# Gate and up projections of an FFN as seven block products for eight, with the gated chunks kept in DRAM until all down projections run last

## What is computed

```python
def swiglu(x, w_gate, w_up, w_down):
    return (jax.nn.silu(x @ w_gate) * (x @ w_up)) @ w_down

def run_trunk(h, p, conv_bufs, past, ...):
    for i in range(DEPTH):
        ...                       # conv mixer or attention, h = h + rmsnorm(y, norm_g[i, 1])
        h = h + rmsnorm(swiglu(rmsnorm(h, norm_g[i, 2]), w_gate[i], w_up[i], w_down[i]), norm_g[i, 3])
        h = h + jax.nn.sigmoid(h @ w_ple_gate[i]) * (p[i] @ w_ple[i])
```

## Time and profile before

| | us |
|---|---|
| median of 3 runs | 3127.33 (3124.76 to 3129.07) |
| span of the profiled execution | 3127.3 |
| TensorE busy | 3075.6 (98%) |
| VectorE busy | 1567.8 (50%) |
| ScalarE busy | 903.5 (29%) |
| GpSimd busy | 262.2 (8%) |
| chain that ended last: TensorE's share | 82% |
| matmuls of the three lines L2273 to L2275 on `xs`, each | 845 to 849 busy |

### The profile page before, as it was taken

How to read it: one execution, slowest core, us unless ns; L and a number is a source line. 1 busy time by engine, 2 the same in 40 slices (tenths; PEclk the granted TensorE clock), 3 DMA queues, 4 the chain that set the end, 5 groups by cost and what they waited for, 6 DMA issues and landing times.

```text
span 3127.3 us, 51548 instructions
## 1 busy us (share of the span) xinstructions
PE 3075.6 (98%) x20352; PEld 2942.6 (94%) x20352; DVE 1567.8 (50%) x2613; ACT 903.5 (29%) x1600; POOL 262.2 (8%) x317
## 2 busy tenths in 40 slices
PE   8999999999999999999999999999999999999999
PEld 8999999999999999999977886569999999999998
DVE  5444284444444447453335665553744444444472
ACT  4111351111111116332235553343411111111262
POOL 1000010000000001000015551110100000000011
PEclk9999999999999999999999999999999999999999
DMA  3111111111111121113257865961111111111112
GB/s 107 45 44 47 42 39 43 48 41 48 46 42 48 41 62 41 41 48 112 98 154 160 162 119 222 395 249 40 42 44 46 48 41 48 41 48 47 57 48 71
DMA packets 229210, 247.46 MB, mean 79 GB/s; under 512 B 19061, under 2 KB 183925, under 8 KB 228994
## 3 DMA queue, kind: packets, MB, share of 16 engines
q1 hardware_dynamic: 204978, 164.65, 17.7%
q0 software_dynamic: 24016, 79.77, 8.3%
...
## 4 chain that ended last, share of the span: by engine, by line
PE 82%; DVE 4%; issue 2%; ACT 1%; DMA 1%; POOL 0%; SPq 0%; DVEq 0%; ACTq 0%; POOLq 0%
PE psum L2273 20%; PE psum L2275 20%; PE psum L2274 20%; PE psum L2857 2%; PE psum L2299 2%; PE psum L2843 2%; PE psum L2293 2%; PE psum L2294 2%; PE psum L2828 1%; PE psum L2829 1%; PE psum L2796 1%; PE psum L2797 1%; PE psum L2798 1%; PE psum L2922 1%; PE psum L2976 1%
## 5 line engine op out<-in xcount | busy, mean ns | idle before, releaser
L2273 PE MATMUL psum<-xs_hi,w_hi 128*128 128x384 f32 (+1 forms) x2592 | 848.9, 327 | 2.6 <-DVE w_lo L1478 2.4
L2275 PE MATMUL psum<-xs_hi,w_lo 128*128 128x384 f32 (+1 forms) x2592 | 845.5, 326 | 0.0
L2274 PE MATMUL psum<-xs_lo,w_hi 128*128 128x384 f32 (+1 forms) x2592 | 844.9, 326 | 0.0
L2273 PEld LDWEIGHTS psum<-xs_hi,w_hi 128*128 128x128 f32 x2592 | 486.6, 188 | 3.7 <-DVE w_lo L1478 3.7
L2274 PEld LDWEIGHTS psum<-xs_lo,w_hi 128*128 128x128 f32 x2592 | 486.7, 188 | 0.0
L2275 PEld LDWEIGHTS psum<-xs_hi,w_lo 128*128 128x128 f32 x2592 | 486.5, 188 | 0.0
L865 ACT ACTIVATE w_hi<-raw 128x1024 fp32r<-128x1024 f32 x192 | 202.4, 1054 | 618.9 <-DVEq L1501 596.9
L1859 DVE TENSOR_TENSOR y<-y,psum 128x384 f32<-128x384 f32 x528 | 268.8, 530 | 155.2 <-PE psum L2275 155.2
L2275 PE MATMUL psum<-hid_hi,w_lo 128*128 128x384 f32 (+1 forms) x1056 | 346.0, 328 | 0.0
L2273 PE MATMUL psum<-hid_hi,w_hi 128*128 128x384 f32 (+1 forms) x1056 | 345.6, 327 | 0.0
L2274 PE MATMUL psum<-hid_lo,w_hi 128*128 128x384 f32 (+1 forms) x1056 | 345.1, 327 | 0.0
...
## 6 DMA issues: line engine op xcount, KB each, us to landing
kpage<-in_cache_k SPq DMA_DIRECT2D x64, 512.0 KB, 8.5
v_page<-in_cache_v POOLq DMA_DIRECT2D x64, 512.0 KB, 5.8
raw<-in_w_gate SPq DMA_DIRECT2D x44, 512.0 KB, 3.7
raw<-in_w_up SPq DMA_DIRECT2D x44, 512.0 KB, 3.7
raw<-in_w_down SPq DMA_DIRECT2D x44, 512.0 KB, 3.8
raw<-in_w_in SPq DMA_DIRECT2D x24, 512.0 KB, 3.6
raw<-in_w_v SPq DMA_DIRECT2D x24, 512.0 KB, 3.4
raw<-in_w_ple_gate SPq DMA_DIRECT2D x16, 512.0 KB, 3.5
```

The lines of the kernel that those rows point to most:

```text
L2273: M(out, wh, xh, start=first, stop=False)
L2274: M(out, wh, xl, start=False, stop=False)
L2275: return M(out, wl, xh, start=False, stop=last)
```

## The change

Groups 2 to 11 of both layers make gate and up by a scheme of Strassen and Winograd. A "unit" is the gate (or the up) of one group: a product of 1024 input features by 256 output features for 1088 tokens. Weights are seen as 2x2 blocks of 512 x 128, inputs as 2x2 blocks of 512 features x 544 tokens. Seven block products (`R11, F2, R12, F3, F1, R22, F4`) replace eight. A product is 2 halves of 272 tokens x 4 chunks x 3 = 24 matmuls, into one of four pairs of PSUM banks in turn (`bank_of`). There are 20 units to a layer (`UNITS`), 40 in all, and 280 products.

New work around them: for each unit GpSimd makes four weight sums and differences in five subtractions or additions of 128x512 (`third_form`, `second_form`, `first_form`, `fourth_form`). ScalarE splits each of the seven weight blocks in a high part in a ring of three (`form_high`), VectorE the low part in place (`form_low`). The products are put together by ScalarE (one copy a unit, `first_part_kept`) and seven additions by VectorE (`part`, 128x544, PSUM plus SBUF). For the gate the two multiplications by `rbB` go to GpSimd (`normed`, `gate_ready`), VectorE keeps those by the sigmoid (`gate_act`) and by up (`hidden`). Once for each layer four combinations of the inputs are made, `t1` to `t4`, each 512 features x 544 tokens: GpSimd scales `h` in 12 instructions of 128x544 and makes five additions or subtractions of 128x2176, ScalarE and VectorE split.

The product of gate and up no longer stays in SBUF: SP stores it to DRAM (`hid_dram`) a quarter at a time, and after the last unit the eleven down projections run one after the other, with a chunk pair of 1.1 MB loaded for each (`hidden(g)`), split by one ScalarE copy and one VectorE subtraction of 128x2176. The first group's contribution to `y` is a copy, so `y` isn't zeroed. Some semaphores are shared to stay within their number.

The diff, cut to its core:

```diff
+R11, F2, R12, F3, F1, R22, F4 = range(7)
+PRODUCTS = 7
+RING = 3
...
+    MOVING = ((xs_hi[:, 0:4, 0:HALF], xs_lo[:, 0:4, 0:HALF]), (t2_hi, t2_lo),
+              (xs_hi[:, 4:8, 0:HALF], xs_lo[:, 4:8, 0:HALF]), (t3_hi, t3_lo), (t1_hi, t1_lo), (t4_hi, t4_lo),
+              (xs_hi[:, 4:8, HALF:T], xs_lo[:, 4:8, HALF:T]))
...
             def ffn(layer):
 
                 pool.wait_ge(h_dve, 6 * layer + 6)
-                pool.memset(y[:, :, :], 0.0).then_inc(y_zero, 1)
+                gained(t3_high, 0, slice(HALF, T))
+                gained(t3_low, 4, slice(HALF, T))
+                pool.wait_ge(t_sum, 8 * layer + 2)
+                G_TT(t3_low[:, :, :], t3_low[:, :, :], t3_high[:, :, :], ALU.subtract).then_inc(t_sum, 1)
+                gained(t1_high, 0, slice(0, HALF))
+                third_form(U0)
+                second_form(U0)
+                first_form(U0)
+                pool.wait_ge(t_sum, 8 * layer + 4)
+                pool.wait_ge(tok_std, TOKS * layer + 2 * NT)
+                G_TT(t2_low[:, :, :], t3_low[:, :, :], t1_high[:, :, :], ALU.add).then_inc(t_sum, 1)
+                G_TT(t1_low[:, :, :], t3_high[:, :, :], t1_high[:, :, :], ALU.subtract).then_inc(t_sum, 1)
+                pool.wait_ge(t_hi, 4 * layer + 2)
+                G_TT(t3_lo[:, :, :], t3_low[:, :, :], t3_hi[:, :, :].bitcast(F32), ALU.subtract).then_inc(t_sum, 1)
+                fourth_form(U0)
+                pool.wait_ge(t_lo, 4 * layer + 2)
+                G_TT(t4_low, t4_low, t2_lo[:, :, :].bitcast(F32), ALU.subtract).then_inc(t_sum, 1)
...
+                def form_high(U, j):
+                    k = PRODUCTS * U + j
...
+                        act_e.wait_ge(product_done, k - RING + 1)
+                    A(high[k % RING][:, :], form[U % 2][j][:, :], ACT.Copy).then_inc(form_hi, 1)
...
+                def unit(U):
+                    first_part_kept(U)
+                    form_high(U, F3)
+                    if not gate:
+                        gate_sigmoid(U // 2, 2)
+                    form_high(U, F1)
...
+                def product(U, j, *waits):
+                    k = PRODUCTS * U + j
+                    pe.wait_ge(form_lo, k + 1)
+                    for w in waits:
+                        pe.wait_ge(*w)
+                    xh, xl = MOVING[j]
+                    for side in range(2):
+                        n = slice(QUAD * side, QUAD * side + QUAD)
+                        for c in range(4):
+                            wc = slice(c * P, (c + 1) * P)
+                            ins = three(psum[:, 2 * bank_of(U, j) + side, 0:QUAD], high[k % RING][:, wc], low[U % 2][j][:, wc],
+                                        xh[:, c, n], xl[:, c, n], c == 0, c == 3)
+                    ins.then_inc(product_done, 1)
...
-                gate_up(n0, b0, True)
-                for g in range(10):
-                    gate_up(n0 + 6 * g + 4, b0 + 12 * g + 4)
-                    down(n0 + 6 * g + 8, b0 + 12 * g + 8, c0 + 2 * g + 2, g % 2)
-                down(n0 + 64, b0 + 124, c0 + 22, 0, True)
+                first_pair(layer)
+                for u in range(2, 4):
+                    slab(n0 + u)
+                    block8(b0 + u, u, n0 + u, xs_hi, xs_lo, None, pre_rows, u - 2, pre_inside)
+                for U in range(U0, U0 + UNITS):
+                    unit(U)
+                for g in range(GROUPS):
+                    down(g)
```

More of the change, by code:

```diff
@@ new lines, in trunk, with form_buffers, at @@
+    t4_hi, t4_lo, t4_low = xs_hi[:, 0:4, HALF:T], xs_lo[:, 0:4, HALF:T], xs_low[:, 0:4, HALF:T]
+    MOVING = ((xs_hi[:, 0:4, 0:HALF], xs_lo[:, 0:4, 0:HALF]), (t2_hi, t2_lo),
+              (xs_hi[:, 4:8, 0:HALF], xs_lo[:, 4:8, 0:HALF]), (t3_hi, t3_lo), (t1_hi, t1_lo), (t4_hi, t4_lo),
+              (xs_hi[:, 4:8, HALF:T], xs_lo[:, 4:8, HALF:T]))
+    def form_buffers(layer):
+        n0 = SLAB0[f"ffn{layer}"]
+        a, b, c = (A_RAW + 4096 * ((n0 + i) % RAWS) for i in range(3))
+        pairs = ((A_STG, A_STG + 4096), (a, A_WH + 4096))
+        sums = {F2: b, F1: b + 2048, F4: c}
+        ring = (c + 2048, A_WH, A_WH + 2048)
+        def at(par, j):
+            return sums[j] if j in sums else pairs[par][j in (F3, R22)] + 2048 * (j in (R12, R22))
+        pair = [[sb(f"pair{layer}_{p}_{i}", [P, 1024], F32, pairs[p][i]) for i in range(2)] for p in range(2)]
+        total = {j: sb(f"form{layer}_{j}", [P, 512], F32, sums[j]) for j in sums}
+        form = [[total[j] if j in sums else pair[p][j in (F3, R22)][:, 512 * (j in (R12, R22)):][:, 0:512]
+                 for j in range(PRODUCTS)] for p in range(2)]
+        low = [[sb(f"form_low{layer}_{p}_{j}", [P, 512], F32R, at(p, j)) for j in range(PRODUCTS)] for p in range(2)]
+        high = [sb(f"form_high{layer}_{i}", [P, 512], F32R, ring[i]) for i in range(RING)]
+        return pair, form, low, high
@@ new lines, in trunk, with raw_of, hi_of, lo_of @@
+    BUFS = [form_buffers(layer) for layer in range(2)]
+    FIRST_DOWN = (SLAB0["dn0"], SLAB0["dn1"])
+    down_raw = sb("down_raw", [P, 1024], F32, A_STG)
+    down_lo = sb("down_lo", [P, 1024], F32R, A_STG)
+    down_hi = sb("down_hi", [P, 1024], F32R, A_STG + 4096)
+    def raw_of(n):
+        return down_raw if n in FIRST_DOWN else raw[n % RAWS]
+    def hi_of(n):
+        return down_hi if n in FIRST_DOWN else w_hi[n % HLS]
+    def lo_of(n):
+        return down_lo if n in FIRST_DOWN else w_lo[n % RAWS]
@@ new lines, in down, with hidden @@
+                def down(g, s):
+                    rows = wd[2 * P * g:2 * P * (g + 1), :].rearrange("(k p) n -> p k n", p=P)
+                    load(dn0 + 2 * g + s, rows[:, :, s * 512:(s + 1) * 512], 2, 512)
+                def hidden(g):
+                    for q in range(4):
+                        sp.wait_ge(hid_stored[q], 16 * (GROUPS * layer + g + 1) + KEY_PAGES * layer)
+                    if g >= HIDS:
+                        sp.wait_ge(acc_ready, NT * (BLK0[f"dn{layer}"] + C * (g - 2)))
+                    elif g:
+                        sp.wait_ge(product_done, PRODUCTS * UNITS * (layer + 1))
+                    else:
+                        sp.wait_ge(product_done, PRODUCTS * (UNITS * (layer + 1) - 1) + 2)
+                    sp.dma_start(hid_raw[g % HIDS][:, :, :],
+                                 hid_dram[layer, 2 * g:2 * g + 2].rearrange("k p t -> p k t"))\
+                        .then_inc(hid_landed[g % HIDS], 16)
@@ L655, in ffn, with gained @@
             def ffn(layer):
-                pool.wait_ge(h_dve, 6 * layer + 6)
-                pool.memset(y[:, :, :], 0.0).then_inc(y_zero, 1)
+                G_TT, G_TS = nc.gpsimd.tensor_tensor, nc.gpsimd.tensor_scalar
+                b0, U0, row = BLK0[f"ffn{layer}"], UNITS * layer, ROW_G + 4 * layer + 2
+                _, form, low, high = BUFS[layer]
+                def gained(dst, c0, cols):
+                    for c in range(4):
+                        ins = G_TS(dst[:, c, :], h[:, c0 + c, cols], vecT[:, c0 + c, row:row + 1], None, ALU.mult)
+                    ins.then_inc(t_sum, 1)
@@ new lines, in form_low, with t_low @@
+                def form_low(U, j):
+                    k = PRODUCTS * U + j
+                    dve.wait_ge(form_hi, k + 1)
+                    dve.wait_ge(forms_made, FORMS * U + {R11: 3, F2: 3, R12: 4, F3: 2, F1: 3, R22: 2, F4: 5}[j])
+                    TT(low[U % 2][j][:, :], form[U % 2][j][:, :], high[k % RING][:, :].bitcast(F32), ALU.subtract)\
+                        .then_inc(form_lo, 1)
+                def t_low(dst, src, hi_part, k):
+                    dve.wait_ge(t_hi, 4 * layer + k)
+                    TT(dst, src, hi_part.bitcast(F32), ALU.subtract).then_inc(t_lo, 1)
@@ new lines, in t4_first, with part @@
+                def t4_first():
+                    dve.wait_ge(acc_ready, NT * (b0 + 4))
+                    dve.wait_ge(t_hi, 4 * layer + 1)
+                    for c in range(4):
+                        ins = V.scalar_tensor_tensor(t4_low[:, c, :], h[:, 4 + c, 0:HALF], vecT[:, 4 + c, row:row + 1],
+                                                     t2_hi[:, c, :].bitcast(F32), ALU.mult, ALU.subtract)
+                    ins.then_inc(t_lo, 1)
+                def part(U, j, out, other):
+                    dve.wait_ge(product_done, PRODUCTS * U + j + 1)
+                    TT(wide(out), product_of(U, j), wide(other), ALU.add).then_inc(part_taken, 1)
```

614 lines of the change are left out of this document (451 added, 163 removed).

## The result

The changed kernel takes 3184.65 us (median of 4 runs, 3179.79 to 3195.38) against 3127.93 us for the kernel before beside it: a ratio of 1.0188, 95% interval 1.0167 to 1.0209. It is slower by 57 us, where 3095 us, 32 us less, was forecast and the range ended at 3140. The profiled execution has a span of 3178.1 us.

The account below looks back on a forecast made before the run. In the feed-forward groups, TensorE's matmul columns were taken as the bound. 3127.3 - 102 (removed matmuls) + 54 (starts) + 10 (unit ends) + 6 (steady state) = 3095 us; range 3038 to 3140.

Parts of the forecast that it names:

- the end of the units: Behind each layer's last product, VectorE's remaining work makes the first down projection wait 5.1 us a layer, 10 us in all.
- Later groups have it under cover: Down projections after the first: VectorE's 17.6 of 23.8 us is hidden, its longest other work 3.6 us against PSUM's 4.9.
- Removed matmuls: Units: seven products at 21.17 us replace two blocks at 23.72; forty units save 102.0 us when TensorE never waits.
- The weight loads: Units: loading weights was predicted not to hold up matmuls of 272 columns, 126.0 ns each.
- The start: Start of each network: TensorE late by 13 us at token sums, 9 at F2, 5 at R22; 27 us a layer, 54.
- A scaling: Network start: GpSimd's scaling of 544 columns taken as 0.8 us, between 0.46 and 1.27, shutting out VectorE's two-SBUF instructions.
- An addition of 2176 columns: Network start: on GpSimd it takes 5.1 us and shuts out VectorE's two-SBUF instructions for its whole length.
- a handful: Network starts: waits may lower TensorE's clock; one earlier wait lost 0.6 us, and a handful was taken as within the range.
- Steady state: Units: GpSimd and VectorE sharing SBUF costs 0.3 us a pair of units, 6 us for 20 pairs.
- Rival B: GpSimd's short instructions cost 1.5 us, 1.6 at 544 columns; 28 us in place of 6, about 3122 us; chance 0.12.
- Rival C: Units: every GpSimd instruction stops VectorE for its whole length; a pair takes 47.7 us, total 3197 us; chance 0.12.

Follow-up runs that it names:

- e1: Changed kernel with the gated-chunk load for a later down group moved behind the current group's second weight slab in SyncE's queue: 3101.34 us, ratio 0.9929.
- e9: Kernel with SyncE's order changed, plus only SyncE's wait for the previous down group's end put back ahead of the second slab: 3121.35 us, ratio 0.9985.
- e7: Kernel before the change, plus unread GpSimd work ahead of its memset (twelve scalings in layer 0; eight scalings, five subtractions in layer 1): 3152.54 us, one run.
- e8: Kernel with only SyncE's order changed, with GpSimd's weight forms in the units replaced by constants or cut to 32 columns: 3094.24 us, ratio 0.9895.

## Why the prediction was wrong

**The step that failed** is the last sentence on the end of the units: "Later groups have it under cover". It puts the down projections at nothing, and they cost 81 us. It counted VectorE's work (17.6 of 23.8 us) and PSUM's cover (4.9 us), which holds: with SyncE's order changed nothing waits (e1). It never followed SyncE's queue, although the new load in it stands in the diff and waits for the end of a group. Read with the order of the queue, the cover is what decides: the slab lands 6.3 us behind the group's end, ScalarE's high and VectorE's low half (which stands first in VectorE's queue) follow, and only then is a bank emptied. The diff's order and the earlier trace rows (3.7 us from issue to landing, with no such load ahead) could have told that a slab comes some 4 us late, which by e9 is worth 17 to 20 us. That a 1088 KB load ahead adds 2.4 us, and with it the rest of the 81, none of the rows showed.

**Removed matmuls, 102 us**: right to the tenth of a microsecond per product (3.026 for 3.02 us). The weight loads did not hold up the short matmuls.

**The start, 54 us**: R22 of the first unit was due at 464.87 + 5 x 3.02 = 480.0, 0.6 later by the run's own offset, and starts at 511.71: 31 us late in layer 0, 32 in layer 1, for 27. The sum is 9 us short, and R22 itself then takes 4.6 and 5.6 us for 3.0 (from its start to F4's, at 516.32 in layer 0), 4 us more in all. The terms are less good than the sum: in layer 0 TensorE is 6, 20 and 31 us late at the last token sum, F2 and R22, where 13, 22 and 27 were forecast. A scaling costs about 1.9 us where the zeros' rate and an addition's bounded it by 0.46 and 1.27: both bounds were from other instructions. But it does not exclude VectorE, as the forecast charged: 12 of them cost TensorE about 1.6 us by themselves (e7). An addition of 2176 columns costs 4.8 to 5.9 us for 5.1 and does exclude it, whole. The 6 us up to the token sums are the 5.27 us for `hs` and small waits; the rest came later, in the chain to R22, as waits of 4.8, 5.5, 4.6 and 2.5 us and a granted clock of 0.85, where 0.6 us was put on a wait's clock and "a handful" taken to be within the range.

**Steady state, 6 us**: nothing was lost. The two engines do hold each other up (VectorE's low parts take 1.2 and 1.1 us on average in place of 0.69, and it is busy for 80% and not 60%), and it stayed hidden (e8). Rival B's prices were met on average, 1.51 us at 512 columns and 1.64 at 544, but as time that includes being held up: the shortest take 1.26 and 1.34, and the units show no wait. Rival C falls: VectorE's excess is 8 us a pair of units (80% of 42.3 less 25.5), half of the 16.8 from which C decides. Its time, 3197, was the nearest to the result; a right number would have had a wrong reason.

**End of the units, 5.1 us a layer**: measured 5.1 twice.

The sum with what was measured, for the two networks: -102 + 63.4 (start) + 4.1 (R22 at the low clock) + 10.2 (end) + 0 (steady) + 81.5 (down projections, the changed kernel's against e1's) = 57 us more, against 58.1 in the table. The forecast had 32 less there, so it missed by 90. The span is only 83 above it because the stretch between the networks came out 7.9 us shorter than before, of which the forecast says nothing and no run here gives the cause.
